# Down projection by seven products for eight, placed inside the next group's first tile, with weight sums on GpSimd

## The chip, the cores and the metric

One NeuronCore of a Trainium2 chip runs the whole program. Its engines are TensorE (PE; PEld is its weight load), VectorE (DVE), ScalarE (ACT), GpSimd (POOL) and the queue of SyncE (SP), which here only issues transfers. The metric is the device time of the program in microseconds.

## The reference

A decoder trunk of two layers on a residual stream H of 1024 tokens by 1024 channels, float32. Layer 0 mixes tokens by pooling, layer 1 by sliding-window attention on a shared K/V. After the mixer each layer has the part that matters here:

```python
def swiglu(x, w_gate, w_up, w_down):
    return (jax.nn.silu(x @ w_gate) * (x @ w_up)) @ w_down

f = swiglu(rms_norm(h, ffn_pre_g[i]), w_ff_gate[i], w_ff_up[i], w_ff_down[i])   # D_FF = 2816
h = h + rms_norm(f, ffn_post_g[i])
gate = sigmoid(rms_norm(h, ple_norm_g[i]) @ w_ple_gate[i])
h = h + (p[i] @ w_ple_proj[i]) * gate
```

## The kernel before

Every float32 product is made of three matmuls on parts: each operand is cut into a high part (`_hi`, a copy to type float32r by ScalarE) and a low part (`_lo`, raw minus high, by VectorE), and hi x hi, hi x lo and lo x hi are added up in PSUM.

The FFN of a layer runs over 11 groups of 256 hidden channels, each of two tiles `t` of 128. For one tile, gate and up projection together are seven products in place of eight (a scheme of the Strassen-Winograd kind, in which sums of blocks are multiplied). The block sums of the weights are called S1 to S4, the plain blocks A11, A12, A22 (A21 only enters sums). `ffn_product` makes one product: 4 x 3 = 12 matmuls of 128x512. The sums of weights are made by VectorE in `form_sum` (L896), their parts by `form_hi` (L776, ScalarE) and `form_lo` (L883, VectorE). `W_RAW` is where a form is loaded or summed; it shares its place with the low part, so it can be loaded again only when its product is done. Results are put together in PSUM by copies (`copy_first`, `copy_m7`, `copy_u`, ScalarE) and additions (`up_first_half`, `up_second_half`, VectorE), then sigmoid (ScalarE) times gate times up (VectorE) gives activations, cut by `act_hi` and `act_lo`.

The down projection follows when a group's two tiles are done: `ffn_pe_down` makes 16 outputs (8 token tiles by 2 halves of the channels), each of two products of three matmuls, in four PSUM banks in turn; VectorE adds each into H (`down`, L1008). The first product of the next group, A11, is put ahead of it. TensorE's order in a group is therefore: S3, S2, A12, S1, A22, S4 of tile 0, the seven of tile 1, A11 of the next group, 16 down outputs.

All engines are programmed by hand, each with its own order of instructions, and wait on semaphores. GpSimd makes only the small reciprocal roots of the norms and some work of the attention. The loads of a form are issued by SP when the product that frees its buffer is counted (`ffn_load_after`); those of A21 wait for a sum. At the end of a layer the additions to H alternate with the post-norm (`ffn_post`), the norm of the next stage (`normed`) and the cutting of its weights (`gate_cut`).

Of the kernel before, what the change touches and what calls it, by code (L numbers as in the profile page):

```python
# [22 lines left out]
P = 128  # L23
# [66 lines left out]
def trunk(nc, I, out):  # L90
    ctx = ExitStack()
    with ctx:
# [48 lines left out]
        gain = sb("gain", [P, D])  # L141
# [10 lines left out]
        def at(kib, *tensors):  # L152
# [6 lines left out]
        Z = region("Z", 184 * KIB,  # L159
# [14 lines left out]
                      ("s1_hi", FORM, F32R), ("s1_lo", FORM, F32R), ("s2_hi", FORM, F32R), ("s2_lo", FORM, F32R),
                      ("s3_hi", FORM, F32R), ("s3_lo", FORM, F32R), ("s4_hi", FORM, F32R), ("s4_lo", FORM, F32R),
                      ("silu0", [P, HALF], F32), ("silu1", [P, HALF], F32)),
                   at(26, ("a11_raw", FORM, F32)), at(30, ("a12_raw", FORM, F32)), at(162, ("a22_raw", FORM, F32)), at(24, ("o_first_hi", [P, KD, P], F32R), ("o_first_lo", [P, KD, P], F32R)),
# [398 lines left out]
        def pool_normed(dve, i, p):  # L576
# [4 lines left out]
            else:  # L581
# [13 lines left out]
        W_RAW = {"A11": Z["a11_raw"], "A12": Z["a12_raw"], "A22": Z["a22_raw"], "S1": Z["s1_raw"], "S2": Z["s2_raw"],  # L595
                 "S3": Z["s3_raw"], "S4": Z["s4_raw"], "A21": Z["a21_raw"]}
        wd, wd_raw = (Z["wd_hi"], Z["wd_lo"]), Z["wd_raw"]
        ffn_a = (Z["ffn_a_hi"], Z["ffn_a_lo"])
        silu, m7, up1 = [Z["silu0"], Z["silu1"]], Z["m7"], Z["up1"]

        F = {
# [1440 lines left out]
```

## Time and profile before

| what | us |
|---|---|
| median of 3 runs | 2053.27 (2048.46 to 2055.6) |
| the profiled execution's own time | 2056.85 |
| its span, first to last instruction | 2055.1 |
| TensorE busy | 1983.0 (96%) |
| VectorE, ScalarE, GpSimd busy | 1330.7, 750.5, 161.1 |
| mean granted TensorE clock | 0.987 |

A busy TensorE is one with matmuls in flight, and these overlap: a matmul of 128x512 is listed with 0.39 us, but the next one starts much earlier. The distance of starts is what counts. A row "A <- B" in a list of waits says that A stood idle until B ended. For VectorE and ScalarE too, the listed duration is some 0.08 us longer than the distance of two that follow each other at once.

### The profile page before, as it was taken

What the parts mean: (1) busy time and instruction counts of PE and PEld (TensorE: products, weight loads), DVE (VectorE), ACT (ScalarE), POOL (GpSimd) and SP (SyncE); (2) the same over time, 40 slices, a digit from 0 to 9 for tenths busy, and PEclk for the clock granted to TensorE, in tenths of its full rate; (3) what the DMA queues carried; (4) which work ended last, traced back from release to release, by engine and by line L of the source; (5) the groups of instructions that cost most, each with busy time, mean ns of one, the idle gap of its engine ahead of it and who ended that gap; (6) DMA issues with size and microseconds to landing.
All of it is one profiled execution on the core that took longest, in us unless ns stands there. A gap on an engine that the chain in (4) does not pass through costs nothing.

```text
span 2055.1 us, 27329 instructions
## 1 busy us (share of the span) xinstructions
PE 1983.0 (96%) x9412; PEld 1631.3 (79%) x9412; DVE 1330.7 (65%) x2126; ACT 750.5 (37%) x1402; POOL 161.1 (8%) x218
## 2 busy tenths in 40 slices
PE   6789999999999999999999997999999999999999
PEld 6668888888888878888866686788888888888887
DVE  5885666666566667477578657666566666655763
ACT  4552222333222243343268644333222233322431
POOL 2200000000000011110036311000000000000110
PEclk8999999999999999999999998999999999999999
DMA  5232222233232251231000112233232223323402
GB/s 187 99 106 93 89 79 87 77 102 97 82 92 78 86 194 37 67 108 52 0 11 2 52 52 97 82 103 97 82 92 77 86 77 102 97 82 106 170 11 82
DMA packets 214756, 173.25 MB, mean 84 GB/s; under 512 B 8608, under 2 KB 196384, under 8 KB 214688
## 3 DMA queue, kind: packets, MB, share of 16 engines
q1 hardware_dynamic: 212960, 166.08, 25.6%
q10 hardware_dynamic: 1728, 6.29, 0.9%
q8 instruction: 40, 0.66, 0.1%
q14 instruction: 28, 0.23, 0.0%
HBM read 159.75 MB, written 12.58 MB: 84 GB/s over the span
## 4 chain that ended last, share of the span: by engine, by line
PE 89%; DVE 6%; POOL 2%; issue 1%; DMA 1%; ACT 1%; SPq 0%; DVEq 0%; ACTq 0%
PE ps L285 15%; PE ps L287 15%; PE ps L286 15%; PE ps L690 13%; PE ps L692 13%; PE ps L691 13%; POOL probs L1352 1%; PE ps L346 1%; DVE ps L1317 1%; PE ps L1306 1%; PE ps L1360 1%; PE ps L563 1%; DVE t_lo L933 1%; PE ps L467 1%; DMA H<-in_x 0%
## 5 line engine op out<-in xcount | busy, mean ns | idle before, releaser
L1008 DVE TENSOR_TENSOR H<-H,ps 128x512 f32<-128x512 f32 x320 | 218.0, 685 | 142.2 <-PE ps L287 142.2
L285 PE MATMUL ps<-wd_hi,ffn_a_hi 128*128 128x512 f32 x704 | 275.1, 391 | 2.4 <-DVE H L1008 1.8
L287 PE MATMUL ps<-wd_hi,ffn_a_lo 128*128 128x512 f32 x704 | 274.6, 390 | 0.0
L286 PE MATMUL ps<-wd_lo,ffn_a_hi 128*128 128x512 f32 x704 | 274.5, 390 | 0.0
L690 PE MATMUL ps<-t_hi,s_hi 128*128 128x512 f32 x528 | 207.7, 393 | 16.8 <-DVE t_lo L933 16.1
L691 PE MATMUL ps<-t_lo,s_hi 128*128 128x512 f32 x528 | 207.0, 392 | 0.0
L692 PE MATMUL ps<-t_hi,s_lo 128*128 128x512 f32 x528 | 206.9, 392 | 0.0
L776 ACT ACTIVATE s_hi<-s_raw 128x512 fp32r<-128x512 f32 x176 | 111.1, 633 | 228.3 <-DVE s_raw L896 225.0
L896 DVE TENSOR_TENSOR s_raw<-s_raw,a_raw 128x512 f32<-128x512 f32 x88 | 60.8, 691 | 191.1 <-DMA s_raw<-in_w_ff_gate 143.6
L800 ACT ACTIVATE m<-ps 128x512 f32<-128x512 f32 x44 | 25.9, 589 | 405.0 <-PE ps L692 405.0
L285 PEld LDWEIGHTS ps<-wd_hi,ffn_a_hi 128*128 128x128 f32 x704 | 132.6, 188 | 31.4 <-issue 4.0
L287 PEld LDWEIGHTS ps<-wd_hi,ffn_a_lo 128*128 128x128 f32 x704 | 132.4, 188 | 27.7
L286 PEld LDWEIGHTS ps<-wd_lo,ffn_a_hi 128*128 128x128 f32 x704 | 132.6, 188 | 27.4
L690 PE MATMUL ps<-b_hi,a_hi 128*128 128x512 f32 x352 | 138.1, 392 | 1.3 <-ACT ps L794 1.3
L691 PE MATMUL ps<-b_lo,a_hi 128*128 128x512 f32 x352 | 137.6, 391 | 0.0
L692 PE MATMUL ps<-b_hi,a_lo 128*128 128x512 f32 x352 | 137.4, 390 | 0.0
L883 DVE TENSOR_TENSOR s_lo<-s_raw,s_hi 128x512 fp32r<-128x512 f32 x176 | 121.4, 690 | 19.3 <-ACT s_hi L776 15.4
L690 PEld LDWEIGHTS ps<-t_hi,s_hi 128*128 128x128 f32 x528 | 100.2, 190 | 38.9 <-DVE t_lo L933 17.0
L692 PEld LDWEIGHTS ps<-t_hi,s_lo 128*128 128x128 f32 x528 | 100.1, 190 | 21.0
L691 PEld LDWEIGHTS ps<-t_lo,s_hi 128*128 128x128 f32 x528 | 100.2, 190 | 20.8
L1043 POOL TENSOR_TENSOR small<-small 128x1 f32<-128x1 f32 x16 | 12.6, 789 | 1318.6 <-ACT ffn_junk L1035 1316.9
L776 ACT ACTIVATE a_hi<-a_raw 128x512 fp32r<-128x512 f32 x132 | 82.3, 625 | 56.3 <-DMA a_raw<-in_w_ff_gate 54.6
(208 smaller groups left out, 4183.3 us busy)
## 6 DMA issues: line engine op xcount, KB each, us to landing
a_raw<-in_w_ff_gate SPq DMA_DIRECT2D x88, 256.0 KB, 2.9
a_raw<-in_w_ff_up SPq DMA_DIRECT2D x88, 256.0 KB, 3.0
s_raw<-in_w_ff_up SPq DMA_DIRECT2D x88, 256.0 KB, 2.9
s_raw<-in_w_ff_gate SPq DMA_DIRECT2D x88, 256.0 KB, 3.0
wd_raw<-in_w_ff_down SPq DMA_DIRECT2D x44, 512.0 KB, 4.2
residual_spill<-H SPq DMA_DIRECT2D x16, 512.0 KB, 2.6
raw<-in_w_ple_gate SPq DMA_DIRECT2D x16, 512.0 KB, 5.7
back<-residual_spill SPq DMA_DIRECT2D x16, 512.0 KB, 6.9
```

The costliest lines, as they stand in the source:

```text
L285: pe.matmul(out_, lhs[0], rhs[0], start=first, stop=False)
L286: pe.matmul(out_, lhs[0], rhs[1], start=False, stop=False)
L287: return pe.matmul(out_, lhs[1], rhs[0], start=False, stop=last)
L346: last = pe.transpose(banks(0)[:, k * P:(k + 1) * P], xn[p][:, k * P:(k + 1) * P], ident[:, :])
L690: pe.matmul(ps[:, bank, :], w[0], x[0], start=fresh and k == 0, stop=False, skip_group_check=not fresh)
L691: pe.matmul(ps[:, bank, :], w[0], x[1], start=False, stop=False, skip_group_check=not fresh)
L692: last = pe.matmul(ps[:, bank, :], w[1], x[0], start=False, stop=k == 3, skip_group_check=not fresh)
L776: act.activation(W[name][0][:, :, :], W_RAW[name][:, :, :], ACT.Copy).then_inc(F["form_hi"], 1)
L800: act.activation(m7[:, :], ps[:, 3, :], ACT.Copy).then_inc(F["copied"], 1)
L883: dve.tensor_tensor(W[name][1][:, :, :], W_RAW[name][:, :, :], W[name][0][:, :, :].bitcast(F32), ALU.subtract).then_inc(F["form"], 1)
L896: dve.tensor_tensor(w, w, W_RAW[other][:, :, :], op).then_inc(F["form_sum"], 1)
L1008: dve.tensor_tensor(dst, dst, ps[:, 4 + n % 4, :], ALU.add).then_inc(F["summed"][n % 4], 1)
```

## The change

The down projection, too, is made by seven products for eight. For each group and each half of the tokens (`h`, four token tiles), a 2x2 block product of activations (blocks: two quarters of tokens by two tiles of hidden channels) with down weights (blocks: two tiles by two channel halves) takes seven block products; a block of activations has 256 tokens, so each product comes twice (j = 0, 1). That is 14 entries of three matmuls in the list `DOWN`. The sums that this takes:

- of down weights: four sums `wd_sums` of 128x512, seven slots, high parts `wd_his` by ScalarE, low parts `wd_los`, all sums and low parts by GpSimd;
- of activations: `d_sums` (four of 128x256 per half, VectorE), `d_his` (ScalarE), `d_los` (VectorE);
- of results: four copies between banks per half (`d_copy_first`, `d_copy_u`, ScalarE) and 12 additions into H (`d_adds`), where there were 8.

The down halves of group g-1 stand inside tile 0 of group g: half 0 behind S3, half 1 behind S1. The last group's halves come behind its last tile. The weight sums S1 to S4 of the gate and up forms go from VectorE to GpSimd, in the order S3, S1, S2, S4, and S2's sum is put in A21's buffer. Silu is one operation of ScalarE, in place of sigmoid and a product. The row of gains of the next stage shares its place with the late activations `act_late`, so it is loaded at the layer's end.

```diff
-        def ffn_load_down(sp, L, g):
-            sp.wait_ge(F["down"], 1 + 16 * (GROUPS * L + g))
...
+        def ffn_load_down(sp, L, g):
+            sp.wait_ge(F["down"], PRODUCTS * (half_of(L, g, 0) + 1))
+            for t in range(2):
+                sp.dma_start(wd_raw[:, 2 * t:2 * t + 2, :].rearrange("p c n -> p (c n)"),
+                             I["w_ff_down"][L][bass.ds((2 * g + t) * P, P), :]).then_inc(F["wd_loaded"][t], 16)
+
+        def ffn_load_tile(sp, L, g, t):
+
+            if not is_first(g, t):
+                ffn_load_after(sp, "S4", "a12", L, g, t, preceding(g, t))
             if not is_last(g, t):
                 n = following(g, t)
                 ffn_load_after(sp, "A11", "a11", L, *n, (g, t))
                 sp.wait_ge(F["form_sum"], nth_sum("S4", L, g, t))
+                ffn_load(sp, "A21", "a21", L, *n)
+                for name, source in (("S3", "a11"), ("S2", "a22"), ("A12", "a12"), ("S1", "a22")):
+                    ffn_load_after(sp, name, source, L, *n, (g, t))
+            if t == 0 and not is_first(g, t):
+                ffn_load_down(sp, L, g)
...
+        def ffn_pe_tile(pe, L, g, t):
+
+            n = tau(L, g, t)
+            pe.wait_ge(F["silu"], 1 + 2 * n - 1)
             ffn_product(pe, "A11", L, g, t)
             pe.wait_ge(F["copied"], nth_copy(1, L, *preceding(g, t)))
+            if t == 1:
+                pe.wait_ge(F["summed"], SUMMED * (half_of(L, g, 0) + 1))
             ffn_product(pe, "S3", L, g, t)
+            if t == 0:
+                ffn_pe_down(pe, L, g - 1, 0, (g, t))
             pe.wait_ge(F["copied"], nth_copy(0, L, g, t))
             ffn_product(pe, "S2", L, g, t)
             ffn_product(pe, "A12", L, g, t)
             pe.wait_ge(F["copied"], nth_copy(2, L, g, t))
             ffn_product(pe, "S1", L, g, t)
+            if t == 0:
+                ffn_pe_down(pe, L, g - 1, 1, (g, t))
             ffn_product(pe, "A22", L, g, t)
             pe.wait_ge(F["up1"], 1 + n + 1)
             ffn_product(pe, "S4", L, g, t)
...
+        DOWN = (("S3", 0, 7), ("A11", 0, 4), ("A11", 1, 3), ("S3", 1, 6), ("A12", 0, 4), ("S2", 0, 5), ("A12", 1, 3),
+                ("S2", 1, 7), ("S1", 0, 5), ("A22", 0, 6), ("S1", 1, 7), ("S4", 0, 5), ("A22", 1, 3), ("S4", 1, 7))
...
+        def ffn_act_tile(act, L, g):
+
+            t, p, n, down = 0, preceding(g, 0), following(g, 0), g - 1
+            gate_silu(act, L, *p, 1)
+            form_hi(act, "S2", L, g, t)
+            d_his(act, L, down, 0)
+            copy_first(act, L, g, t)
+            copy_m7(act, L, g, t)
+            form_hi(act, "A12", L, g, t)
+            for j in range(2):
+                d_copy_first(act, L, down, 0, j)
+            form_hi(act, "S1", L, g, t)
+            for j in range(2):
+                d_copy_u(act, L, down, 0, j)
...
+        def ffn_act_second(act, L, g):
+
+            t, p, n = 1, (g, 0), following(g, 1)
+            gate_silu(act, L, *p, 1)
+            copy_first(act, L, g, t)
+            form_hi(act, "A22", L, g, t)
+            form_hi(act, "S4", L, g, t)
+            copy_m7(act, L, g, t)
+            wd_his(act, L, g, (0, 1))
+            copy_u(act, L, g, t)
+            wd_his(act, L, g, (2, 3))
...
+        def form_sum(pool, name, L, g, t):
+
+            other, op = {"S3": ("A21", ALU.subtract), "S1": ("A21", ALU.add), "S2": ("S3", ALU.subtract),
+                         "S4": ("S2", ALU.subtract)}[name]
+            pool.wait_ge(F["form_loaded"][name], 16 * (tau(L, g, t) + 1))
+            if name == "S4":
+                pool.wait_ge(F["form"], nth("S2", L, g, t))
...
+        def wd_sums(pool, L, g):
+
+            r = GROUPS * L + g
+            slot = [wd_raw[:, k, :] for k in range(7)]
+            pool.wait_ge(F["wd_loaded"][0], 16 * (r + 1))
+            pool.tensor_tensor(slot[4], slot[1], slot[0], ALU.subtract).then_inc(F["wd_sum"], 1)
+            pool.wait_ge(F["wd_loaded"][1], 16 * (r + 1))
...
+        def wd_los(pool, L, g):
+            r = GROUPS * L + g
+            for k in range(7):
+                if k % 2 == 0:
+                    pool.wait_ge(F["wd_hi"], 4 * r + k // 2 + 1)
+                if k == 0:
+                    pool.wait_ge(F["wd_sum"], 4 * r + 4)
+                pool.tensor_tensor(wd_lo[:, k, :], wd_raw[:, k, :], wd_hi[:, k, :].bitcast(F32), ALU.subtract
+                                   ).then_inc(F["wd"], 1)
...
+        def ffn_pool(pool, L, g):
+            n1, n2 = (g, 1), (g + 1, 0)
+            if not is_first(g, 0):
+                form_sum(pool, "S4", L, g, 0)
+            for name in ("S3", "S1", "S2"):
+                form_sum(pool, name, L, *n1)
+            wd_sums(pool, L, g)
+            form_sum(pool, "S4", L, *n1)
+            if not is_last(*n1):
+                form_sum(pool, "S3", L, *n2)
+            wd_los(pool, L, g)
+            if not is_last(*n1):
+                for name in ("S1", "S2"):
+                    form_sum(pool, name, L, *n2)
...
         def form_lo(dve, name, L, g, t):
             dve.wait_ge(F["form_hi"], nth(name, L, g, t))
+            if name == "S3":
+                dve.wait_ge(F["form_sum"], nth_sum("S2", L, g, t))
...
+        def ffn_dve_tile(dve, L, g, first_group=False):
+
+            t, p, n, down = 0, preceding(g, 0), following(g, 0), g - 1
+            times_up(dve, L, *p, 1)
+            form_lo(dve, "S2", L, g, t)
+            d_los(dve, L, down, 0)
...
+            d_adds(dve, L, down, 0, first_group)
+            form_lo(dve, "A12", L, g, t)
+            d_sums(dve, L, down, 1)
+            form_lo(dve, "S1", L, g, t)
+            d_los(dve, L, down, 1)
+            form_lo(dve, "A22", L, g, t)
+            form_lo(dve, "S4", L, g, t)
+            d_adds(dve, L, down, 1, first_group)
+            up_second_half(dve, L, g, t)
+            form_lo(dve, "A11", L, *n)
+            form_lo(dve, "S3", L, *n)
+            up_first_half(dve, L, g, t)
+            times_up(dve, L, g, t, 0)
+            form_lo(dve, "S2", L, *n)
+
+        def ffn_dve_second(dve, L, g):
+
+            t, p, n = 1, (g, 0), following(g, 1)
+            times_up(dve, L, *p, 1)
+            for name in ("A12", "S1", "A22", "S4"):
+                form_lo(dve, name, L, g, t)
+            if not is_last(g, t):
+                form_lo(dve, "A11", L, *n)
+            up_second_half(dve, L, g, t)
+            up_first_half(dve, L, g, t)
+            times_up(dve, L, g, t, 0)
+            d_sums(dve, L, g, 0)
+            if not is_last(g, t):
+                form_lo(dve, "S3", L, *n)
```

## Rows read from the trace of the kernel before

**Rows 1.** Head of the page: span, and the clock granted to TensorE in 40 slices
```profile
span 2055.1 us, 27329 instructions
...
PEclk8999999999999999999999998999999999999999
```

**Rows 2.** TensorE's waits from 152 to 749 us (total, times, longest)
```profile
PE ps L285 <- issue: 0.3, 1, 0.3
```

**Rows 3.** Timeline of TensorE at two group ends (start, us, instruction)
```profile
411.94 0.39 PE L690 MATMUL ps<-t_hi,s_hi 128*128 128x512 f32 x1
...
414.66 0.39 PE L690 MATMUL ps<-t_hi,s_hi 128*128 128x512 f32 x1
...
471.78 0.39 PE L690 MATMUL ps<-t_hi,s_hi 128*128 128x512 f32 x1
```

**Rows 4.** Groups by line and shape (busy us, mean ns, idle before)
```profile
L1008 DVE TENSOR_TENSOR H<-H,ps 128x512 f32<-128x512 f32 x320 | 218.0, 685 | 142.2 <-PE ps L287 142.2
L883 DVE TENSOR_TENSOR s_lo<-s_raw,s_hi 128x512 fp32r<-128x512 f32 x176 | 121.4, 690 | 19.3 <-ACT s_hi L776 15.4
L1153 DVE TENSOR_TENSOR pT_lo<-p_raw,pT_hi 128x256 fp32r<-128x256 f32 x16 | 6.6, 414 | 0.0
L776 ACT ACTIVATE s_hi<-s_raw 128x512 fp32r<-128x512 f32 x176 | 111.1, 633 | 228.3 <-DVE s_raw L896 225.0
L780 ACT ACTIVATE wd_hi<-wd_raw 128x1024 fp32r<-128x1024 f32 x44 | 46.0, 1045 | 0.0
```

**Rows 5.** Timeline, how one engine follows another
```profile
414.94 0.60 ACT L800 ACTIVATE m<-ps 128x512 f32<-128x512 f32 x1 [20.25 <-PE ps L692]
...
426.43 0.68 DVE L925 TENSOR_TENSOR m<-ps,m 128x512 f32<-128x512 f32 x1
427.21 0.69 DVE L910 TENSOR_TENSOR silu<-m,silu 128x512 f32<-128x512 f32 x1
427.82 0.68 DVE L883 TENSOR_TENSOR s_lo<-s_raw,s_hi 128x512 fp32r<-128x512 f32 x1
```

**Rows 6.** Loads: SP's queue, their landing times, and a sum that waits for one
```profile
412.30 0.90 SPq L679 DMA_DIRECT2D wd_raw<-in_w_ff_down  x2
...
433.02 0.68 DVE L896 TENSOR_TENSOR s_raw<-s_raw 128x512 f32<-128x512 f32 x1
...
437.56 0.69 DVE L896 TENSOR_TENSOR s_raw<-s_raw,a_raw 128x512 f32<-128x512 f32 x1 [1.86 <-DMA s_raw<-in_w_ff_gate]
...
DMA to landing us min/median/max: 3.5/4.2/5.0
```

**Rows 7.** GpSimd's two-input operations: groups, and L327's range in ns
```profile
L1428 POOL TENSOR_TENSOR o_first_lo<-qo,o_first_hi 128x1024 fp32r<-128x1024 f32 x1 | 2.4, 2362 | 0.0
L327 POOL TENSOR_TENSOR small<-small x56: 190/218/1183, 7.6 to 2016.2; 128x1 f32<-128x1 f32 x56
```

**Rows 8.** Timeline: VectorE and GpSimd at the same time
```profile
1147.81 1.89 POOL L1352 TENSOR_TENSOR probs<-probs,recip 128x1024 f32<-128x1024 f32 x1 [1.22 <-DVE recip L1344]
...
1148.38 2.40 DVE L280 TENSOR_TENSOR w_o_lo<-raw,w_o_hi 128x1024 fp32r<-128x1024 f32 x1
...
757.95 1.23 DVE L1059 TENSOR_TENSOR H<-H,back 128x1024 f32<-128x1024 f32 x1
...
757.99 1.59 POOL L1047 TENSOR_TENSOR small<-small 128x1 f32<-128x1 f32 x1 [2.83 <-DVE H L1055]
761.63 0.55 POOL L329 TENSOR_TENSOR small<-small 128x1 f32<-128x1 f32 x1
```

**Rows 9.** DMA issues, last column us to landing
```profile
gain<-in_ple_norm_g ACTq DMA_DIRECT2D x2, 512.0 KB, 4.4
```

**Rows 10.** Timeline of TensorE after two long waits
```profile
110.47 0.79 PE L690 MATMUL ps<-t_hi,s_hi 128*128 128x512 f32 x1 [7.70 <-DVE t_lo L933]
...
111.49 0.63 PE L692 MATMUL ps<-t_hi,s_lo 128*128 128x512 f32 x1
...
93.91 1.07 PE L467 MATMUL ps<-ident,tmp 128*128 128x128 f32 x8 [3.30 <-DVE b_lo L517]
```

More of the change, by code:

```diff
@@ L174, in trunk @@
[L174 to L177, printed above, removed]
@@ L594, in trunk @@
              "S4": xb["b22"]}
[L595 to L599, printed above, removed]
+        W_RAW = {n: Z[f"{n.lower()}_raw"] for n in ORDER + ("A21",)}
+        m7, act_late = Z["m7"], ACT_LATE
@@ L856, in ffn_act_rest @@
             n = following(g, t)
+            for name in ("A11", "S3", "S2", "A12", "S1"):
+                form_hi(act, name, L, *n)
+        def ffn_act_tile(act, L, g):
+            t, p, n, down = 0, preceding(g, 0), following(g, 0), g - 1
+            gate_silu(act, L, *p, 1)
+            form_hi(act, "S2", L, g, t)
+            d_his(act, L, down, 0)
[8 more added lines that the diff above has]
+            form_hi(act, "A22", L, g, t)
+            form_hi(act, "S4", L, g, t)
+            copy_u(act, L, g, t)
+            d_his(act, L, down, 1)
+            form_hi(act, "A11", L, *n)
+            for j in range(2):
+                d_copy_first(act, L, down, 1, j)
+            form_hi(act, "S3", L, *n)
+            for j in range(2):
+                d_copy_u(act, L, down, 1, j)
+            gate_silu(act, L, g, t, 0)
+            for name in ("S2", "A12", "S1"):
+                form_hi(act, name, L, *n)
@@ new lines, in d_adds @@
+        def d_adds(dve, L, g, h, first_group=False, between=None):
+            u, bank_of, begun = half_of(L, g, h), {x[:2]: x[2] for x in DOWN}, set()
+            for k, (name, j, q, c) in enumerate(ADDS):
+                dve.wait_ge(F["down"], nth_down(name, j, u))
+                n = 4 * h + 2 * q + j
+                dst, src = H[:, n * D + c * HALF:n * D + (c + 1) * HALF], ps[:, bank_of[name, j], :]
+                if first_group and (n, c) not in begun:
+                    begun.add((n, c))
+                    dve.tensor_copy(dst, src).then_inc(F["summed"], 1)
+                else:
+                    dve.tensor_tensor(dst, dst, src, ALU.add).then_inc(F["summed"], 1)
+                if between:
+                    between(k)
@@ L1487, in spill_tile @@
                     sp.dma_start(spill[L][:, j * D:(j + 1) * D], H[:, j * D:(j + 1) * D]).then_inc(F["spilled"], 16)
-                first, second = (0, 0), (0, 1)
+                first = (0, 0)
                 if L == 1:
@@ L1493, in ffn_loads @@
                 ffn_load(sp, "A12", "a12", L, *first)
+                if L == 1:
+                    sp.wait_ge(F["form_sum"], nth_sum("S4", 0, GROUPS - 1, 1))
+                ffn_load(sp, "A21", "a21", L, *first)
                 for j in range(5):
@@ L1497, in ffn_loads @@
                     sp.wait_ge(s["lo"][0], s.done("lo", PAIRS - 1))
-                ffn_load(sp, "A21", "a21", L, *first)
                 ffn_load(sp, "S2", "a22", L, *first)
```

563 lines of the change are left out of this document (290 added, 273 removed).

## The prediction

> **What bounds the kernel now.** I read the page first: TensorE is busy nearly everywhere, and its granted clock is full in all but a few slices [rows 1]. The question is then whether it ever waits in the feed-forward (FFN) stages. The list of waits, cut to 152 to 749 us of layer 0, answers it: 0.3 us in 597 [rows 2]. So there the number of matmuls sets the time, whatever the others do. The timeline of TensorE gives the price: the same product (S3 of a tile) starts at 411.94 and again at 471.78, one group of 264 matmuls later. A group is 59.84 us, a matmul 0.2267 us; a product of 12 takes 2.72 [rows 3]. All other engines have room: one group has 54 VectorE operations of about 0.69 us and two of twice that, some 39.7 us, and ScalarE 14 of 0.63, 14 of 0.60 and two of 1.05, some 19 us [rows 4, 5]. GpSimd does nothing in these stages. The change spends this room, so the second question is not how much room there is, but how long the new chains through the other engines are.
>
> **What is removed from TensorE.** The down projection had 96 matmuls in a group (16 x 2 x 3), and gets 84 (2 halves x 14 x 3). That is 12 x 22 groups = 264 matmuls, 264 x 0.2267 = 59.8 us less. It is certain if nobody keeps TensorE waiting. A group is then 57.12 us.
>
> **What VectorE and ScalarE get.** VectorE loses 8 sums of weight forms, 4 gate products, 4 low parts of activations and the two wide low parts of the down weights; it gets 8 more additions into H, 8 quarter sums, and 9 low parts (5 wide, 4 narrow): 51 x 0.69 + 12 x 0.41 = 40.1 us of 57.1 [rows 4]. ScalarE rises to about 28 us: per group 8 more copies between banks (0.60 each [rows 5]), 3.8 us for seven slots of weights (by 1.045 for two [rows 4]), and narrower pieces. Both fit. I also followed the twelve additions inside a down half against its 14 products of 0.68 us: an addition starts 0.2 us after its product, back to back additions cost 0.61 [rows 5], and each bank comes free about 0.5 us before the product that wants it. So I cost the inside of a down half at nothing; the cover is 0.5 us in 9.5, thin. Silu for sigmoid times gate: nothing, ScalarE has the room; a table load at each switch of function would be hidden there too. The bytes loaded are the same; on SP the two down loads now stand behind the S1 form's load and ahead of A22's, which finds its product (32.64 to 35.36 below) later than they are issued, so nobody is held up by them.
>
> **What GpSimd gets.** 19 two-input operations of 128x512 per group. The trace has none of this size. One of 128x1024 took 2.362 us and one of a single column 0.190 [rows 7]; the line through both gives 1.28 for 512 columns. Below, half of 2.362 is 1.18; above, with the 0.55 us that a power of one column takes [rows 8] as the fixed part, 1.46. I take 1.28: both of its rows are the same operation. 19 x 1.28 = 24.3 us fits into 57.1. But GpSimd and VectorE exclude each other. VectorE's w_o_lo, with two inputs in SBUF, took 2.40 us at 1148.38 beside a GpSimd multiply that ran to 1149.70; alone it takes 1.22, so it really began at 1149.56, when the multiply was nearly over. The reverse: at 757.99 a power on GpSimd took 1.59 in place of 0.55, beside a two-input VectorE operation that ended at 759.18 [rows 8]. From these a GpSimd and a VectorE operation of 512 columns take 1.28 + 0.69 - 0.14 - 0.15 = 1.68 us as a pair; two on GpSimd alone 1.25 each. A waiting VectorE operation that gets in between thus costs GpSimd 0.43, a narrow one 0.16. Additions with an input in PSUM are free of this.
>
> The Trainium skill (SBUF — State Buffer, "Who interferes with whom") calls it an exclusive lock, held for the whole instruction; the trace agrees but for the 0.14 us. With full exclusion the nine pairs below would cost 0.29 more each, and the time would be near 2134. The Trainium skill (GPSIMD Engine Reference, "Engine selection") advises against two-input elementwise work there, at 1.96 times VectorE's time; by that a sum is 1.35 us as an estimate, and the time near 2106.
>
> **The new chain.** Take t = 0 at A11 of a group, and TensorE undisturbed: S3 at 2.72, down half 0 at 5.44 to 14.96, S2, A12, S1 to 23.12, down half 1 to 32.64, A22, S4 to 38.08; second tile S3 at 40.80, S4 ends at 57.12.
> 1. The down weights of this group can only be loaded when the previous group's last down product is read: 32.64. SP issues 0.36 us later (411.94 to 412.30) and they land after 3.5 and, issued second, up to 5.0 [rows 3, 6]: 36.5 and 38.2.
> 2. GpSimd's queue has the four down sums, then S4 of the second tile. The first gets in at 36.8, the next at 38.5, behind VectorE's S2 low part. Four operations with three of VectorE's between them (times_up, two low parts): 38.5 + 4 x 1.28 + 3 x 0.4 = 44.8.
> 3. The load of A21 waits for that S4 sum, and S3's stands behind it on SP. Before, such a pair let the next sum start 3.86 us after the end of the sum that it waited for (433.70 to 437.56) [rows 6]. So 48.65.
> 4. Then GpSimd has S3, seven down low parts, S1, S2: 1.28 + 9 x 1.25 = 12.5. VectorE has two wide operations and four quarter sums there: 2 x 0.43 + 4 x 0.16 = 1.5. End 62.7.
> 5. VectorE's low part of S3 waits for the sum S2, since both use S3's raw buffer; 0.69 and two short handovers (427.11 to 427.21 is one [rows 5]), together 0.8, later TensorE may start S3 of the next group: 63.5. It wants to at 57.12 + 2.72 = 59.84. **A stall of 3.65 us**, and about 0.15 more where the down half's second form waits behind times_up, S2's low part and a GpSimd sum. Behind that low part on VectorE stand times_up, S2's low part and the forms of the down half, so these are no earlier.
>
> The chain closes on itself (S3, down half 1, load), so each group takes 57.1 + 3.8 = 60.9 us against 59.84: the saved 2.72 is lost and 1.1 more. There are 9 such passages in a layer (into groups 2 to 10), 18 x 3.8 = 68.4. Into group 1 step 1 is missing, since the weights are loaded early: I get 1.9, twice 3.8.
>
> **The end of a layer.** The last group's down halves have no tile around them. Half 0 waits for silu (0.28 us after the last product, 414.66 to 414.94 [rows 3, 5], + 0.58), a high part and two operations on VectorE: 2.3. Half 1 waits until VectorE has ended the additions and made four quarter sums and a low part: 3.4. The additions to H share VectorE with post-norm work that had 21.8 us of down projection to hide in and has 19 less dense ones; and the gain row, which now shares its buffer with late activations, is loaded only after them, 4.4 us [rows 9], while VectorE stands at the norm that needs it with additions queued behind. I take 5 us for these two (bounds 1 and 9). Together 10.7, twice 21.4. At the start of a layer VectorE loses four sums (4 x 0.61) and GpSimd's four can each hold it up: zero, within 3 either way.
>
> **Sum.** -59.8 + 68.4 + 3.8 + 21.4 = +33.8 us. The profiled execution took 2056.85 (span 2055.1), 3.6 above the median; so 2056.85 + 33.8 - 3.6 = 2087.
>
> **Rivals.** The result turns on the stall per passage: it breaks even at (59.8 - 25.2) / 18 = 1.92 us.
> - *Little collision (faster).* GpSimd's operations find VectorE on additions or idle, and neither is held up. Step 2 ends at 43.1, step 4 at 59.5, the stall is 0.5, no stall into group 1: -59.8 + 9 + 21.4 = -29.4, 2024. With 1.18 us per operation no stall is left: 2015. For it: 28 of VectorE's 63 operations, 19 us of 40, have an input in PSUM and are free of the exclusion. Against it: steps 2 and 4 lie just where VectorE makes low parts and sums, and the rows of two-input pairs are plain. Chance 0.30, both together.
> - *GpSimd slower (worse).* With 1.46 us, 15 operations in the chain add 2.7 per passage: 2087 + 18 x 2.7 + 4 = 2140. The clock points the same way: after a wait of 7.7 us a matmul at 111.49 took 0.63 in place of 0.39, the level of 1.2 GHz; after one of 3.3 us it did not fall [rows 10]. Stalls of 4 us lie between. Chance 0.17.
> - *Even.* A stall near 1.9 us: 0.08.
> - The forecast, 2050 to 2115 for its own range: 0.45.
>
> A measurement here tells about 0.3%, 6 us, from no change. Faster 0.30, same 0.08, slower 0.62. The range goes 10 us below the 2015 of the fastest variant and stops 12 short of 2140: 2005 to 2128. It leaves out the rest of the slow case and a saving without any loss at the layer's end.
>
> **What would show it.** TensorE should have one wait per group, of 3 to 4 us, at the first matmul of S3 of the first tile, released by VectorE's low part; GpSimd busy without a break in the 12 to 14 us before it. Rows of GpSimd at 128x512 should read 1.28 us where alone and more beside low parts, and VectorE's low parts should have a maximum near 1.8. If these means stay near 0.69 and the wait is missing, the lock is what I had wrong; if TensorE waits inside the down halves, it is the 0.5 us of cover. The matmul count must fall by 264. I would be wrong most simply if GpSimd's operation is much under 1.28.

## The result and the profile after

The changed kernel takes 2143.5 us (median of 4 runs, 2140.17 to 2145.53) against 2053.93 for the kernel before in the same comparison: 1.0439 times, 95% interval 1.0416 to 1.0463. It is slower, by 90 us where 34 were forecast, and lies outside the range. The profiled execution took 2140.17 us; it is compared with the profiled one of before, 2056.85, so +83.3. All times here and below are of fast runs.

The head of the page gives a span of 2138.4 us. Its clock row of 40 slices is no different from that of before [rows 1], since a 9 there stands for 90% or more; that row, which I read as full, can't show a loss of this size. The mean granted clock over the whole span is 0.964, where it was 0.987. The windows view of 152 to 749 us, in the FFN of layer 0, shows the difference (PE busy first, the granted clock is the third last number); the first row is of the kernel before, the second of the changed one:

```profile
span 2138.4 us, 28715 instructions
...
152.00:749.00 597.00, 596.70 (x2633) 493.81 (x2632) 373.62 (x551) 177.05 (x294) 0.00 (x0) 1.00 0.31 95
...
152.00:749.00 597.00, 559.53 (x2369) 458.21 (x2370) 454.34 (x602) 235.47 (x429) 250.85 (x175) 0.96 0.27 82
```

The list of TensorE's waits over the whole span (total, times, longest) has a new first line. Before there was nothing of this kind inside the FFN [rows 2]:

```profile
PE ps L721 <- DVE s_lo L1028: 77.5, 20, 4.2
...
PE ps L801 <- DVE d_ac_lo L1077: 11.0, 4, 3.2
...
PE ps L288 <- DVE H L1104: 5.4, 2, 2.7
```

L721 to L723 are the matmuls of `ffn_product`, L801 to L803 those of the down products, L1028 is `form_lo`, L978 `form_sum` on GpSimd, L1001 `wd_los`. There are 20 waits of 3.9 us for the low part of S3, one for each passage from group to group: the place and the releaser that the prediction named. One passage in the timeline, the engines put together (start, us, instruction, idle before):

```profile
313.40 0.89 SPq L694 DMA_DIRECT2D wd_raw<-in_w_ff_down  x2
...
317.42 1.72 POOL L986 TENSOR_TENSOR wd_raw<-wd_raw 128x512 f32<-128x512 f32 x1 [8.13 <-DMA wd_raw<-in_w_ff_down]
...
320.98 1.77 DVE L1028 TENSOR_TENSOR a_lo<-a_raw,a_hi 128x512 fp32r<-128x512 f32 x1
...
322.67 1.77 DVE L1028 TENSOR_TENSOR s_lo<-s_raw,s_hi 128x512 fp32r<-128x512 f32 x1
323.86 1.74 POOL L978 TENSOR_TENSOR s_raw<-s_raw,a_raw 128x512 f32<-128x512 f32 x1
...
329.47 1.29 POOL L978 TENSOR_TENSOR s_raw<-s_raw,a_raw 128x512 f32<-128x512 f32 x1 [3.87 <-DMA s_raw<-in_w_ff_gate]
...
330.72 10.04 POOL L1001 TENSOR_TENSOR wd_lo<-wd_raw,wd_hi 128x512 fp32r<-128x512 f32 x7
340.73 1.44 POOL L978 TENSOR_TENSOR s_raw<-s_raw,a_raw 128x512 f32<-128x512 f32 x1
342.25 1.32 POOL L978 TENSOR_TENSOR a_raw<-s_raw 128x512 f32<-128x512 f32 x1
...
343.61 0.69 DVE L1028 TENSOR_TENSOR s_lo<-s_raw,s_hi 128x512 fp32r<-128x512 f32 x1 [1.15 <-POOL a_raw L978]
...
344.35 0.80 PE L721 MATMUL ps<-t_hi,s_hi 128*128 128x512 f32 x1 [3.92 <-DVE s_lo L1028]
344.94 0.63 PE L722 MATMUL ps<-t_lo,s_hi 128*128 128x512 f32 x1
```

Read it downwards: load of the down weights, four down sums and S4 (to 325.60), loads (3.87), S3, seven low parts, S1, S2 without a break, the low part, S3's matmul. The last line is the news: the matmul behind the wait takes 0.63 us where [rows 3] have 0.39. The windows view gives the granted clock of the 5 us behind this wait, and of 10 us a little later:

```profile
344.50:349.50 5.00, 5.00 (x12) 3.98 (x13) 4.29 (x6) 2.08 (x5) 1.57 (x1) 0.50 0.17 49
351.00:361.00 10.00, 10.00 (x46) 8.26 (x45) 8.39 (x14) 3.92 (x7) 1.30 (x1) 1.00 0.09 26
```

TensorE is busy all the time in both, but at 0.50, the level of 1.2 GHz, it does 12 matmuls in 5 us, one in 0.427 in place of 0.227. From the wait at 344.35 it takes 13 matmuls until it is back at full rate (at 349.93; 13 would have taken 2.95 us and took 5.58: 2.6 lost), behind the next one, at 408.37, it takes 7 (at 411.38: 1.4 lost). So it is behind all 20 waits, mostly by turns 1.4 to 1.8 and 2.4 to 2.9 us lost, together 40.8: every passage costs its wait and then 2.0 us more.

The groups by line and shape show what the pairs of engines cost each other (busy us, mean ns). Before, a low part took 690 ns [rows 4]:

```profile
L978 POOL TENSOR_TENSOR s_raw<-s_raw,a_raw 128x512 f32<-128x512 f32 x132 | 195.6, 1483 | 583.0 <-DMA s_raw<-in_w_ff_up 333.1 <-DMA s_raw<-in_w_ff_gate 186.1 <-DVE s_lo L1028 63.8
...
L1001 POOL TENSOR_TENSOR wd_lo<-wd_raw,wd_hi 128x512 fp32r<-128x512 f32 x154 | 218.6, 1455 | 4.3 <-ACT wd_hi L863 4.3
...
L1028 DVE TENSOR_TENSOR a_lo<-a_raw,a_hi 128x512 fp32r<-128x512 f32 x132 | 151.4, 1148 | 83.5 <-ACT a_hi L851 83.5
```

### The profile page after: what moved, and what is told of

It reads as the page before. It is cut to its first block, busy times and chain, and to the rows that moved or that the text cites. A ratio compares the mean times of both kernels' runs of the same rounds, so it can differ in the third digit from the quotient of the medians.

```text
span 2138.4 us, 28715 instructions
## 1 busy us (share of the span) xinstructions
PE 1977.8 (92%) x9150; PEld 1612.4 (75%) x9150; DVE 1555.4 (73%) x2280; ACT 901.0 (42%) x1734; POOL 764.1 (36%) x636
## 4 chain that ended last, share of the span: by engine, by line
PE 58%; POOL 19%; DMA 8%; issue 7%; DVE 7%; ACT 1%; SPq 0%; POOLq 0%; DVEq 0%; ACTq 0%
POOL wd_lo L1001 9%; PE ps L288 7%; PE ps L289 7%; PE ps L290 7%; PE ps L801 6%; PE ps L803 6%; PE ps L802 6%; PE ps L721 5%; PE ps L722 5%; PE ps L723 5%; DMA wd_raw<-in_w_ff_down 4%; POOL s_raw L978 3%; DMA a_raw<-in_w_ff_up 3%; POOL wd_raw L990 2%; POOL a_raw L978 1%
## 5 line engine op out<-in xcount | busy, mean ns | idle before, releaser
L1104 DVE TENSOR_TENSOR H<-H,ps 128x512 f32<-128x512 f32 x496 | 328.0, 686 | 113.0 <-PE ps L803 112.9
L978 POOL TENSOR_TENSOR s_raw<-s_raw,a_raw 128x512 f32<-128x512 f32 x132 | 195.6, 1483 | 583.0 <-DMA s_raw<-in_w_ff_up 333.1
L721 PE MATMUL ps<-t_hi,s_hi 128*128 128x512 f32 x528 | 226.2, 428 | 93.2 <-DVE s_lo L1028 77.5
L723 PE MATMUL ps<-t_hi,s_lo 128*128 128x512 f32 x528 | 220.5, 418 | 0.0
L1001 POOL TENSOR_TENSOR wd_lo<-wd_raw,wd_hi 128x512 fp32r<-128x512 f32 x154 | 218.6, 1455 | 4.3 <-ACT wd_hi L863 4.3
L1028 DVE TENSOR_TENSOR a_lo<-a_raw,a_hi 128x512 fp32r<-128x512 f32 x132 | 151.4, 1148 | 83.5 <-ACT a_hi L851 83.5
L721 PEld LDWEIGHTS ps<-t_hi,s_hi 128*128 128x128 f32 x528 | 108.8, 206 | 127.7 <-DVE s_lo L1028 86.0
L1028 DVE TENSOR_TENSOR s_lo<-s_raw,s_hi 128x512 fp32r<-128x512 f32 x132 | 116.7, 884 | 36.4 <-POOL a_raw L978 33.4
L721 PE MATMUL ps<-b_hi,a_hi 128*128 128x512 f32 x352 | 138.4, 393 | 2.0 <-ACT ps L878 1.3
L801 PE MATMUL ps<-wd_hi,d_ab_hi 128*128 128x512 f32 x352 | 138.8, 394 | 0.9 <-ACT ps L818 0.9
L802 PE MATMUL ps<-wd_lo,d_ab_hi 128*128 128x512 f32 x352 | 138.5, 393 | 0.0
L803 PE MATMUL ps<-wd_hi,d_ab_lo 128*128 128x512 f32 x352 | 138.2, 393 | 0.0
L723 PE MATMUL ps<-b_hi,a_lo 128*128 128x512 f32 x352 | 137.8, 392 | 0.0
L723 PEld LDWEIGHTS ps<-t_hi,s_lo 128*128 128x128 f32 x528 | 108.7, 206 | 24.6
L722 PEld LDWEIGHTS ps<-t_lo,s_hi 128*128 128x128 f32 x528 | 109.4, 207 | 22.5
L851 ACT ACTIVATE s_hi<-s_raw 128x512 fp32r<-128x512 f32 x132 | 82.6, 626 | 69.0 <-POOL s_raw L978 69.0
L288 PE MATMUL ps<-w_ple_gate_hi,xt_hi 128*128 128x512 f32 x256 | 103.2, 403 | 5.4 <-DVE H L1104 5.4
L289 PE MATMUL ps<-w_ple_gate_lo,xt_hi 128*128 128x512 f32 x256 | 101.5, 396 | 0.0
```

The lines of the kernel that those rows point to most:

```text
L288: pe.matmul(out_, lhs[0], rhs[0], start=first, stop=False)
L289: pe.matmul(out_, lhs[0], rhs[1], start=False, stop=False)
L721: pe.matmul(ps[:, bank, :], w[0], x[0], start=fresh and k == 0, stop=False, skip_group_check=not fresh)
L722: pe.matmul(ps[:, bank, :], w[0], x[1], start=False, stop=False, skip_group_check=not fresh)
L723: last = pe.matmul(ps[:, bank, :], w[1], x[0], start=False, stop=k == 3, skip_group_check=not fresh)
L801: pe.matmul(ps[:, bank, :], a[0], wd_hi[:, b, :], start=fresh, stop=False, skip_group_check=not fresh)
```

## The experiments

All medians are of 4 to 10 runs beside runs of the kernel before on the same chip (2054.5 to 2054.7 there). "Theory" is: the GpSimd chain makes a wait of 4 us, and the clock falls behind it. Kernels e1 to e4 and e7 to e11 start from the changed kernel, e5 and e6 from the one before.

**e1: the sums S1 and S2 ahead of the last three low parts.**

```python
-            wd_los(pool, L, g)
+            wd_los(pool, L, g, range(4))
...
                 for name in ("S1", "S2"):
                     form_sum(pool, name, L, *n2)
+            wd_los(pool, L, g, range(4, 7))
```

> GpSimd makes the sums S1 and S2 of the next tile ahead of the last three of the seven down low parts, instead of behind them; nothing else differs from the changed kernel. Theory A (one long chain through GpSimd sets the group time): the low part of S3 is ready three GpSimd operations earlier (3 x 1.25 to 1.7 us), so the wait of about 4 us at the first matmul of S3 goes; a wait of 0.5 to 1.2 us appears instead at the first down product, which wants all seven low parts; no wait long enough to lower the clock is left; a group takes 57.6 to 58.4 us instead of 63.2, the whole 2143 - 18 x 5.2 = 2050, between 2040 and 2060. Theory B (VectorE, with 40 us of work and the collisions, is the limit of a group): the order on GpSimd doesn't matter, the group stays at 62 to 63.5 us and the time at 2120 or more.

Measured: 2137.59, 1.0400 (1.0372 to 1.0428). A miss: 6 us gained of 90. The timeline, VectorE, GpSimd and TensorE:

```profile
336.66 1.30 DVE L1067 TENSOR_TENSOR d_ac_raw<-d_ab_raw 128x256 f32<-128x256 f32 x1
337.89 1.51 DVE L1068 TENSOR_TENSOR d_ac_raw<-d_ab_raw 128x256 f32<-128x256 f32 x1
...
342.16 1.75 DVE L1029 TENSOR_TENSOR s_lo<-s_raw,s_hi 128x512 fp32r<-128x512 f32 x1
...
337.76 1.35 POOL L978 TENSOR_TENSOR a_raw<-s_raw 128x512 f32<-128x512 f32 x1
339.08 4.29 POOL L1001 TENSOR_TENSOR wd_lo<-wd_raw,wd_hi 128x512 fp32r<-128x512 f32 x3
...
343.97 0.80 PE L721 MATMUL ps<-t_hi,s_hi 128*128 128x512 f32 x1 [3.54 <-DVE s_lo L1029]
```

The sum S2 is ready at 339.11, 4.5 us sooner than in the changed kernel, as meant. But S3's low part stands on VectorE behind four quarter sums, and each of these takes 1.3 to 1.5 us in place of 0.41, and the timeline has a GpSimd operation between every two. Two chains, one on GpSimd and one on VectorE, ended within about a microsecond of each other; e1 shortened one of them.

**e2: 16 spare matmuls in the wait.** They go into a free PSUM bank and nothing reads it; the rest is computed as before.

```python
+            else:   # tile 0, ahead of S3
+                for _ in range(16):
+                    pe.matmul(ps[:, 4, :], W["A12"][0][:, 0, :], X["A12"][0][:, :, 0, :], start=True, stop=True)
```

> TensorE makes 16 spare matmuls of 128x512 into an unused bank ahead of S3 in the first tile of each group: 3.6 us of work that the output doesn't use, inside its wait of 4.1 us. Theory A with the clock as its second part (each wait costs itself plus about 2 to 2.4 us, because the granted clock falls to half behind it): the granted clock stays full, the first matmuls of S3 come at 0.227 us distance instead of 0.43, S3 starts as late as before, and a group takes 61.0 to 61.4 us instead of 63.2: 2143 - 18 x 2.0 = 2107, between 2098 and 2115. Theory C (the clock falls for another reason, the lower activity of the whole group): the clock goes on falling, the time stays within 2135 to 2150.

Measured: 2105.7, 1.0251 (1.0220 to 1.0281). TensorE's timeline, and below it 60 us (about one group) by windows:

```profile
335.22 3.79 PE L764 MATMUL ps<-b_hi,a_hi 128*128 128x512 f32 x16
339.18 0.50 PE L721 MATMUL ps<-t_hi,s_hi 128*128 128x512 f32 x1 [0.17 <-DVE s_lo L1031]
339.52 0.39 PE L722 MATMUL ps<-t_lo,s_hi 128*128 128x512 f32 x1
...
212.00:272.00 60.00, 59.65 (x264) 48.87 (x263) 47.02 (x63) 24.85 (x45) 26.33 (x19) 1.00 0.28 84
```

The same window of after has 235 matmuls at a clock of 0.94. S3 starts as late as its low part lets it, and yet the kernel is 37.8 us faster with more work in it: a group takes 61.4 us, the clock falls in none of the 20 passages, and what it cost is 37.8 us, 1.9 for each. This is the experiment that separates the length of a wait from its price. The spare matmuls also raise the activity of the whole group, so e2 alone leaves Theory C open; e7 below has none of them and keeps most of the clock too.

**e3: the low parts of the down weights by VectorE.**

```python
-            wd_los(pool, L, g)
...
+            wd_los(dve, L, g, range(4))          # in ffn_dve_second, ahead of A11's low part
...
             up_second_half(dve, L, g, t)
+            wd_los(dve, L, g, range(4, 7))
```

> The seven low parts of the down weights are made by VectorE, in its second tile, where it stood idle; GpSimd keeps all sums. Theory A: GpSimd's chain behind the A21 load shrinks from ten operations to three, which wait only for their loads; S3's low part is ready before TensorE wants it, no wait is left at S3, a group takes 57.2 to 57.6 us, the whole about 2143 - 18 x 5.8 = 2039, between 2030 and 2050, although VectorE has 4.3 us more work per group. Theory B (VectorE is the limit): 4 us more per group, 2143 + 77 = 2220.

Measured: 2028.25, 0.9864 (0.9836 to 0.9892), a little better than the range given: no wait at S3 is left, and the kernel is faster than the one before by 26 us, 1.4%. A group takes 57.5 us. One window as above, and the waits at the end of layer 0:

```profile
212.00:272.00 60.00, 59.93 (x265) 49.10 (x264) 51.65 (x75) 26.47 (x48) 17.94 (x12) 1.00 0.32 96
...
724.80 0.49 PE L801 MATMUL ps<-wd_hi,d_ac_hi 128*128 128x512 f32 x1 [2.10 <-DVE d_ac_lo L1076]
739.40 0.76 PE L801 MATMUL ps<-wd_hi,d_ac_hi 128*128 128x512 f32 x1 [3.19 <-DVE d_ac_lo L1076]
749.74 0.50 PE L801 MATMUL ps<-wd_hi,d_ac_hi 128*128 128x512 f32 x1 [0.31 <-ACT ps L825]
756.23 0.80 PE L288 MATMUL ps<-w_ple_gate_hi,xt_hi 128*128 128x512 f32 x1 [2.59 <-DVE H L1103]
```

VectorE is busy 51.65 of 60 us and still has no part in any wait of the steady groups; GpSimd falls to 18. In this case the busier engine is the better place: GpSimd's chain behind the A21 load falls from ten operations to three.

**e4: the fourth down sum made twice** (the same result again, one more GpSimd operation in the chain).

```python
+            pool.tensor_tensor(slot[6], slot[2], slot[5], ALU.subtract).then_inc(F["again"], 1)
+            pool.wait_ge(F["again"], r + 1)
             pool.tensor_tensor(slot[6], slot[2], slot[5], ALU.subtract).then_inc(F["wd_sum"], 1)
```

> GpSimd makes the fourth down sum twice, one operation of 128x512 more per group, in the chain ahead of the sum S4. Theory A: each passage gets longer by one GpSimd operation, 1.3 us alone or 1.7 with a VectorE operation in between: the wait at S3 grows from 4.1 to 5.4 to 5.8 us, the time by 18 x 1.3 to 18 x 1.7, 23 to 31 us, and a little more for the clock: 2166 to 2180. Theory B: GpSimd is busy 40% of a group and has room, so the time stays within 2138 to 2150.

Measured: 2178.35, 1.0602 (1.0573 to 1.0631), the time as expected: 35 us for 22 operations, 1.6 each. The place is not. The list of waits, and one of the new waits with what stands ahead of it on ScalarE:

```profile
PE ps L721 <- DVE s_lo L1030: 80.9, 21, 4.2
PE ps L721 <- ACT ps L888: 28.1, 22, 1.7
...
333.04 0.63 ACT L851 ACTIVATE s_hi<-s_raw 128x512 fp32r<-128x512 f32 x1 [4.43 <-POOL s_raw L978]
...
336.66 0.49 PE L721 MATMUL ps<-t_hi,s_hi 128*128 128x512 f32 x1 [1.14 <-ACT ps L888]
```

The S3 wait does not grow. The added operation makes the sum S4 later, ScalarE waits for that sum, and behind it on ScalarE stands the copy (L888) that the product S1 of the second tile needs; so TensorE waits there first, and has that much less to wait at S3. The chain closes on itself, and a wait on it may show at more than one place.

**e5 and e6: two parts of the change alone, in the kernel before.** In e5 the weight sums of the gate and up forms go from VectorE to GpSimd (`ffn_pool`); in e6 ScalarE makes silu, in place of a sigmoid and a product by VectorE.

```python
-                form_sum(dve, "S3", L, *n)
-                form_sum(dve, "S2", L, *n)
...
+        def ffn_pool(pool, L, g, tiles):
+            for t in tiles:
+                for name in SUMS:
+                    form_sum(pool, name, L, g, t)
```

> The kernel before, with one part of the change alone: the eight weight sums of a group are made by GpSimd instead of VectorE, in the same order; the down projection stays with 16 outputs of six matmuls. Theory A (what hurts is not GpSimd's slowness or its collisions as such, but a chain of 15 such operations between two loads that TensorE waits for): here at most two or three sums stand one behind another and VectorE loses 8 operations, so TensorE hardly waits in a group, 59.84 us as before, the time within 0.5% of 2054 (2045 to 2064). Theory D (the exclusion of GpSimd and VectorE hurts wherever both work): each of 16 sums in two tiles holds up a form's low part by 1 us, waits appear at several products of each tile, and the time is 2075 or more.

```python
-            act.activation(silu[h][:, :], ps[:, h, :], ACT.Sigmoid).then_inc(F["sig"], 1)
+            act.activation(silu[h][:, :], ps[:, h, :], ACT.Silu).then_inc(F["prod"], 1)
...
-            gate_times_sigmoid(dve, L, g, t, 0)
```

> The kernel before, with another part of the change alone: silu as one operation of ScalarE, the product with the gate on VectorE left out. TensorE did not wait in the FFN stages before, so nothing is there to gain: 2054 within 0.3% (2048 to 2060). A ScalarE table load at the switch to the sigmoid of the next stage may show, 1.3 us once or twice a layer, beside other work.

Measured: 2052.75, 0.9994 (0.9983 to 1.0005), and 2051.7, 0.9985 (0.9973 to 0.9997). Neither moves the time by more than 0.3%. Eight sums a group on GpSimd are harmless here; in the changed kernel the eleven operations on the down weights share its queue.

**e7: e1, and S3's low part between the second and third quarter sum.**

```python
-            d_sums(dve, L, g, 0)
+            d_sums(dve, L, g, 0, (0,))
             form_lo(dve, "S3", L, *n)
+            d_sums(dve, L, g, 0, (1,))
```

> The kernel of the run with the sums S1 and S2 ahead of three low parts on GpSimd, and besides VectorE makes the low part of S3 behind the first two quarter sums instead of behind all four. That run kept its wait of 3.6 us, and its trace shows why: the sum S2 was ready 4.5 us earlier, but VectorE stood in the four quarter sums, each drawn out to 1.4 us by a GpSimd operation. Theory A' (two queues that meet: GpSimd's chain and VectorE's quarter sums, which it stretches): S3 starts about 2.8 us earlier, its wait falls to about 1 us; the other two quarter sums come later, so the first down product waits for its activation forms, 1.5 to 2.5 us; both are too short for the clock to fall. A group takes 59.6 to 61 us instead of 63.1, the whole 2137 - 18 x 2.1 to 3.5 = 2074 to 2100. Theory B (VectorE's total work sets the group time): it stays at 2130 to 2140.

Measured: 2119.17, 1.0313 (1.0285 to 1.0341), worse than the range given. VectorE's low part and TensorE's three waits of the passage:

```profile
340.60 1.77 DVE L1029 TENSOR_TENSOR s_lo<-s_raw,s_hi 128x512 fp32r<-128x512 f32 x1
...
342.43 0.50 PE L721 MATMUL ps<-t_hi,s_hi 128*128 128x512 f32 x1 [0.99 <-DVE s_lo L1029]
347.10 0.50 PE L801 MATMUL ps<-wd_hi,d_ac_hi 128*128 128x512 f32 x1 [1.65 <-DVE d_ac_lo L1081]
348.79 0.50 PE L801 MATMUL ps<-wd_hi,d_ab_hi 128*128 128x512 f32 x1 [0.73 <-DVE d_ab_lo L1085]
```

The wait of 3.5 is now 0.99, 1.65 and 0.73, together nearly as long. But the clock mostly stays up: it falls in 4 of the 20 passages (granted 0.99 as a mean from 152 to 700 us, 0.96 in e1; the first matmul takes 0.50 us, not 0.80), which is where the gain is from. A group takes 61.6 us in place of 63.2: 1.6 less, where 2.1 to 3.5 were expected, which is 9 us of the miss. The other 10 were found with e8.

**e8: e3, and at the end of a layer the parts of down half 0 ahead of the last silu and its product.**

```python
+                d_his(act, L, last, 0)
                 gate_silu(act, L, last, 1, 1)
...
+                d_los(dve, L, last, 0)
                 times_up(dve, L, last, 1, 1)
```

> The kernel with the seven low parts of the down weights on VectorE (2028 us), and besides, in the last group of a layer, the forms of the first down half are cut before the last silu and its product with up, on ScalarE and VectorE, instead of behind them. The wait of 2.1 us at the first product of this half was forecast as part of the cost of a layer's end. If that is so, it falls to less than 0.5 us in both layers, 3.5 to 4.5 us in all: 2024 (2020 to 2027). If instead the seven low parts or the additions set that start, the wait only changes its releaser and the time stays at 2028.

Measured: 2031.79, 0.9893 (0.9873 to 0.9913): not faster than e3, and outside the expected range. (The profiled execution, 2037.74, is the longest of the five.) At the layer's end the wait of 2.10 falls to 1.40 only, not below 0.5, but no half clock follows it. From the first tile's end to the gate product, layer 0 is 2.2 us shorter (144.08 to 762.14, in e3 135.98 to 756.23), as meant, but the start of each layer lost more, though its code is that of e3. VectorE, GpSimd and TensorE there:

```profile
115.12 0.69 DVE L1027 TENSOR_TENSOR s_lo<-a_raw,s_hi 128x512 fp32r<-128x512 f32 x1
115.72 2.29 DVE L1113 TENSOR_TENSOR t_lo<-t_raw,t_hi 128x2048 fp32r<-128x2048 f32 x1
...
119.12 2.29 DVE L1113 TENSOR_TENSOR t_lo<-t_raw,t_hi 128x2048 fp32r<-128x2048 f32 x1
...
115.94 6.59 POOL L978 TENSOR_TENSOR s_raw<-s_raw,a_raw 128x512 f32<-128x512 f32 x1 [10.23 <-DVE s_lo L1027]
...
124.27 0.76 PE L721 MATMUL ps<-t_hi,s_hi 128*128 128x512 f32 x1 [3.80 <-issue]
```

One GpSimd sum takes 6.59 us: it begins in the middle of a long VectorE operation, and VectorE then runs through three more two-input operations to 121.41 before it gets in. In e3 the same sum got in after the first of them and took 3.22. The next forms are loaded after that sum, so TensorE stands 3.80 us (3.72 in layer 1), and the clock falls. The profile puts the wait down to "issue"; that it belongs to the sum was at this point a guess from the two timelines. The trace of e7 has the same row (6.59 at 113.93), and both have it in layer 1 too.

**e9: e8, and VectorE waits for that sum; e10: e7 with the same wait; e11: e3 once more.**

```python
             t_lo(1, 3)
+            dve.wait_ge(F["form_sum"], nth_sum("S4", L, g, t))
             form_lo(dve, "S1", L, g, t)
```

> The kernel with the low parts on VectorE and the other order at the layer's end, and at the start of each layer VectorE waits for GpSimd's fourth weight sum (S4) before its low part of S1. In e8 that sum took 6.59 us at 115.94, since VectorE ran from one two-input operation into the next until 121.41; in e3 it got in at 115.3 and took 3.22, and TensorE waited 0.72 in place of 3.80. If this explains why e8 was not faster than e3, the sum takes about 3.2 us again, the wait of 3.8 with nothing to show for it goes to 0.7, and the time is e8's less 2 x 5.5, about 2021 (2017 to 2026). If the reordering at the end was itself the loss, it stays at 2030 to 2034.

> The kernel of e7 (S1 and S2 sums first, S3's low part between the quarter sums, low parts of the down weights still on GpSimd) with the same wait. In e7 the S4 sum took 6.59 us too, and TensorE waited 3.5 and 3.7 us there. If that is worth 5.5 us in a layer, the time is 2119 - 11 = 2108 (2104 to 2112), and e7's gain from ending the long wait is about 30 us, not 18. If it is worth nothing, 2119.

> The kernel of e3 once more, unchanged, on the same chip as e9: 2028 (2025 to 2031), so that the step between them is of the kernels and not of the chip.

Measured on one chip: e9 2023.95, 0.9853 (0.9836 to 0.9869); e10 2108.87, 1.0260 (1.0243 to 1.0277); e11 2028.01, 0.9872 (0.9855 to 0.9888). All three as expected. In e9:

```profile
113.01 3.22 POOL L978 TENSOR_TENSOR s_raw<-s_raw,a_raw 128x512 f32<-128x512 f32 x1 [10.22 <-DVE s_lo L1027]
...
116.27 0.69 DVE L1027 TENSOR_TENSOR s_lo<-s_raw,s_hi 128x512 fp32r<-128x512 f32 x1 [1.19 <-POOL s_raw L978]
...
118.12 0.47 PE L721 MATMUL ps<-t_hi,s_hi 128*128 128x512 f32 x1 [0.72 <-issue]
```

A wait of 1.19 us put into VectorE takes 8 (e9 against e8) to 10 us (e10 against e7) out of the kernel; the runs of e7 and e10 overlap a little (2113.36 to 2122.96, 2106.7 to 2118.32), those of e8 and e9 don't. The sum takes 3.22 us again and TensorE's wait 0.72, so the guess is shown. e9 is also 4.1 us faster than e11, which is what the new order at the layer's end was expected to give. It is the fastest version: 30.6 us below the kernel before.

## Why the prediction was wrong

**Right: what is removed, and the chain.** Where TensorE does not wait a group takes 57.5 us (e3; 57.1 forecast), so nearly all of the 59.8 us are there to be had. The matmul records fall from 9412 to 9150. The chain came out almost as worked out, from the end of the down weights' last use:

| step | forecast, us | measured at 313 to 344 |
|---|---|---|
| end of the last down product to end of the S4 sum | 12.16 | 12.56 |
| load until the S3 sum starts | 3.86 | 3.87 |
| ten GpSimd operations | 14.05 | 14.10 |
| to TensorE's S3 | 0.8 | 0.78 |
| wait of TensorE, start against the start without it | 3.8 | 4.07 |

One GpSimd operation alone takes 1.28 to 1.29 us (1.28 forecast); a pair with VectorE repeats after 1.69 (320.98, 322.67; 1.68 forecast). That silu and the sums of the gate and up forms on GpSimd cost nothing by themselves is shown by e5 and e6, that the inside of a down half in the steady groups has no wait by the list of waits, which from 160 to 700 us has the wait at S3 alone. Additions with an input in PSUM are free of GpSimd, as taken: they took 0.69 us beside it (124 of them) and without it.

**Wrong: the price of a wait.** The step that failed is "each group takes 57.1 + 3.8 = 60.9 us". S3 of tile 0 starts at 154.34 and, nine groups later, at 723.69: 63.26 each, 63.13 in layer 1. The waits are 4.07 of the 6.1 above 57.12; the other 2.0 are matmuls at half clock behind them. I had seen a matmul at 0.63 us behind a wait of 7.7 and none behind one of 3.3 [rows 10], wrote that waits of 4 lie between, and then gave it no money in the forecast and mentioned it only beside a rival. e2 measured it directly: 37.8 us. The trace of the kernel before had rows that speak against the one of 3.3, and I did not look at them. Behind a wait of 1.82 us at the end of layer 0 TensorE starts at full rate and falls to half 1.2 us later, for 3.4 us (0.50 granted from 761.20 to 764.40):

```profile
759.92 0.47 PE L285 MATMUL ps<-wd_hi,ffn_a_hi 128*128 128x512 f32 x1 [1.82 <-DVE H L1008]
...
761.62 0.63 PE L285 MATMUL ps<-wd_hi,ffn_a_hi 128*128 128x512 f32 x1
```

One of 1.90 at 1288.77 does the same. So the length of a wait alone does not decide it, and half clock behind waits of 4 us was to be reckoned with before any run. The Trainium skill (TensorE: Matmul & The Clock Gate, "HAM oscillation — how this bites in real kernels") describes a kernel in which a wait in every turn of the loop brings the clock down in every turn, so that the price is paid each time and not once; by that, the trace agrees, with 20 falls behind 20 waits. In e7, where each turn has three short waits, it fell in 4 of 20.

**Too small: the passage into group 1.** I took 1.9 us since the down weights are loaded early there. The weights are early, but the four down sums stand on GpSimd behind S1 and S2 of the second tile and start at 127.30; S4 ends at 135.39, and the load (3.98) and the ten operations follow as everywhere. The waits are 4.18 and 3.98, like all others, and have their half clock too: some 12.0 us for the two, not 3.8.

**Right as a sum by luck, not in its parts: the ends of the layers.** The waits for the forms of the down halves are 2.29 and 3.19 (forecast 2.3 and 3.4); for the rest, 5 us, there are 0.33 and 2.70 (and 0.9 for a copy in layer 1). The clock fills the difference. In e3, where nothing else waits, the first down half with its wait takes 14.60 us (724.80 to 739.40) where 42 matmuls and 3.19 of wait make 12.7, and the second 16.83 in place of 12.4; the gate and projection products behind take 17.1 (756.23 to 773.34) where before they took 14.5 (773.44 to 787.94). So waits of 8.2 us cost about 17 in a layer, less a microsecond or two won at its start, and less the 3.4 us that the kernel before itself lost at the end of layer 0.

The account against the profiled executions, forecast and measured: matmuls -59.8 and -59.8 (by their number); 18 passages +68.4 and +109.4; two into group 1 +3.8 and +12.0; the ends, with all else, +21.4 and +21.7 (what is left). Together +33.8 and +83.3. By the medians the whole is +89.6 and the rest 28, so the closeness of 21.4 and 21.7 says nothing.

**The rivals.** The case "little collision" fell with the first row of the waits. "GpSimd slower" had the right total, 2140, for the wrong reason: its operation takes 1.28, not 1.46. By the Trainium skill (SBUF — State Buffer, "Who interferes with whom") the two exclude each other for the whole instruction; I put that at 0.29 us more for each of the nine pairs, by listed durations. By the distances of starts, which count, 1.25 us for GpSimd (329.47 to 330.72) and 0.61 for VectorE [rows 5], the estimate is 1.86 for a pair, 0.18 more than I took. The measured 1.69 agrees with the row I used and not with that. The ratio of 1.96 that I gave from the Trainium skill (GPSIMD Engine Reference) stands there under "Elementwise — side-by-side cycle accounting"; for 512 columns the trace has 1.28 to 0.69, 1.86. My break-even of 1.92 us of wait was for a wait that costs its own length alone. e10 against e1 shows the other price once more: 3.4 us of wait per passage in three pieces, or 3.5 in one, and 28.7 us between them, though in e10's profiled execution, the longest of its four, the clock still fell in 7 of 20.

**What my first repair missed.** e1 was expected to win 90 us and won 6. I had followed only GpSimd's queue to the low part, and not the four quarter sums ahead of it on VectorE, each stretched from 0.41 to 1.4 us by GpSimd. The prediction had counted them as a delay to GpSimd (4 x 0.16) and not as a delay to VectorE.

**What stays open.** Why VectorE let the GpSimd sum in after one operation in e3 and after four in e8 was not found: in both it begins 0.2 us into the same long low part (113.35 behind 113.14, 115.94 behind 115.72), and the code there is the same. Nor was it found what decides whether the clock falls behind a wait of a given length, and where the last 0.4 us of a group in e3 go. The ends of the layers were not repaired further than e9 does; 29 of the 59.8 us stay lost, most of them there.

## What to carry to other kernels

A wait of TensorE that returns in every turn of a loop can have two prices, its length and the matmuls at half clock behind it: fill it with spare matmuls once, as in e2, to learn which is which. Work moved to GpSimd is not free because GpSimd is idle: count how it stretches VectorE's two-input operations too, and follow both queues to the instruction that TensorE waits for. Where the order of the two engines is left open, a short wait that fixes their order can be worth many times its length.

## What the runs showed of the hardware

- Behind each of the 20 waits of 3.7 to 4.2 us in the changed kernel the granted clock fell to 0.50, for 7 to 14 matmuls, sometimes only 0.9 us after the first of them (154.34). Behind waits of 0.99, 1.65 and 0.73 us in e7 it stayed up in 16 of 20 passages. Between these the length does not decide: half clock followed waits of 1.82 and 1.90 (before), 2.10 and 3.19 (e3, 0.76 us for the matmul at 739.40), and not those of 1.40 (e8) and 3.30 (before) [rows 10].
- A GpSimd operation of 128x512 with two inputs stretches a 128x256 one of VectorE from 0.41 to 1.3 to 1.5 us and a 128x512 one from 0.69 to 1.77; its own time goes from 1.28 to 1.74. Additions of VectorE with an input in PSUM kept their 0.69.
- VectorE can keep a GpSimd operation out over several of its own: 6.59 us for one that takes 1.28 alone.
